# One-token sample projections in plain fp32 column groups, from weights fetched again, in a hybrid decoder layer

## What is computed

```python
def mixer_layer(x, c, start_pos, pool_buf, conv_buf, S0, chunked, ...):
    h = rms_norm(x, pre_norm_w) * (1.0 + scale[:, None]) + shift[:, None]
    proj = h @ w_in                       # 1024 -> 3080 columns
    u_a, z_a, qkv, z_b, b_raw, a_raw = jnp.split(proj, cuts, axis=-1)
    y_a, new_pool = pool_mix(u_a, pool_buf, start_pos, pool_w, pool_scale)
    ...                                   # short conv, gated delta rule, gates
    y = jnp.concatenate([y_a, y_b], axis=-1) @ w_out
    return x + gate[:, None] * rms_norm(y, post_norm_w), ...

yp, ... = mixer_layer(yp, c_prompt, 0, ..., True, *params)    # 2048 rows
ys, ... = mixer_layer(ys, c_sample, PAST_LEN, ..., False, *params)    # 8 rows
```

## Time and profile before

| | before |
|---|---|
| median of 3 runs | 1063.57 us (1062.31 to 1066.26) |
| the profiled execution, its own time | 1062.29 us |
| its span | 1060.5 us |
| TensorE busy | 1017.0 us, 96% |
| TensorE weight loads | 796.3 us, 75% |
| VectorE busy | 669.1 us, 63% |
| ScalarE busy | 363.8 us, 34% |
| GpSimd busy | 218.0 us, 21% |
| mean granted TensorE clock | 0.991 |
| HBM read, written | 156.43 MB, 44.81 MB |

### The profile page before, as it was taken

One profiled execution on the slowest core, in us unless ns is written; L12 is line 12 of the kernel. 1 busy time (PEld: TensorE's weight loads), 2 busy tenths in 40 slices (PEclk: granted clock), 3 DMA queues, 4 the chain that ended last, 5 costly groups with the idle time before them and its releaser, 6 DMA issues.

```text
span 1060.5 us, 16761 instructions
## 1 busy us (share of the span) xinstructions
PE 1017.0 (96%) x6235; PEld 796.3 (75%) x6235; DVE 669.1 (63%) x1392; ACT 363.8 (34%) x725; POOL 218.0 (21%) x222
## 2 busy tenths in 40 slices
PE   4999989999999999999999999999999999999995
PEld 1567667877777788887877788887877888888774
DVE  2479897577356795566356884676256775555644
ACT  5356322433714511322524511314426531121211
POOL 0133345565400101231000102230000100533000
PEclk9989999999999999999999999999999999999998
DMA  9696566364867553243756553244674343322265
GB/s 344 250 363 230 207 221 269 123 221 160 294 223 269 197 195 128 112 159 132 265 184 252 199 198 120 80 178 160 258 283 169 119 159 120 115 80 86 95 233 179
DMA packets 46803, 202.32 MB, mean 191 GB/s; under 512 B 9162, under 2 KB 9930, under 8 KB 29188
## 3 DMA queue, kind: packets, MB, share of 16 engines
q1 hardware_dynamic: 46724, 201.26, 51.8%
HBM read 156.43 MB, written 44.81 MB: 190 GB/s over the span
## 4 chain that ended last, share of the span: by engine, by line
PE 66%; DVE 1%; issue 1%; POOL 1%; ACT 0%; DVEq 0%; POOLq 0%; ACTq 0%
PE acc L2128 13%; PE acc L2130 12%; PE acc L2129 12%; PE ring L2178 9%; PE ring L2165 2%; PE acc L2165 2%; PE ring L2166 2%; PE ring L2167 2%; PE acc L2167 2%; PE acc L2166 2%; PE ring L2195 1%; PE ring L2204 1%; PE ring L2205 1%; PE ring L2365 1%; PE ring L2187 1%
## 5 line engine op out<-in xcount | busy, mean ns | idle before, releaser
L2128 PE MATMUL acc<-hhi,wsl 128*128 128x512 f32 x768 | 317.8, 414 | 4.8 <-DVE y L1367 4.7
L2130 PE MATMUL acc<-hhi,wsl 128*128 128x512 f32 x768 | 301.7, 393 | 0.0
L2129 PE MATMUL acc<-hlo,wsl 128*128 128x512 f32 x768 | 301.4, 392 | 0.0
L2128 PEld LDWEIGHTS acc<-hhi,wsl 128*128 128x128 f32 x768 | 145.7, 190 | 43.6 <-issue 10.6
L2130 PEld LDWEIGHTS acc<-hhi,wsl 128*128 128x128 f32 x768 | 145.1, 189 | 31.9
L2129 PEld LDWEIGHTS acc<-hlo,wsl 128*128 128x128 f32 x768 | 145.5, 189 | 27.8 <-issue 2.2
L1251 DVE SCALAR_TENSOR_TENSOR cacc<-raw,cw,cacc 128x512 f32<-128x512 f32 x144 | 114.8, 797 | 5.1
L1900 POOL TENSOR_TENSOR wsl<-wraw,wsl 128x512 fp32r<-128x512 f32 x60 | 84.1, 1418 | 107.7 <-ACT wsl L901 107.7
L934 ACT ACTIVATE raw<-acc 128x512 f32<-128x512 f32 x48 | 28.6, 597 | 140.6 <-PE acc L2130 140.5
L2165 PE MATMUL acc<-wsl,yhi 128*128 128x512 f32 x128 | 51.4, 401 | 5.0 <-DVE y L1367 3.4
L1248 DVE TENSOR_SCALAR cacc<-raw,cw 128x512 f32<-128x512 f32 x48 | 25.4, 529 | 47.1 <-ACT raw L934 44.3
(11 more groups left out here) (323 smaller groups left out, 1668.2 us busy)
## 6 DMA issues: line engine op xcount, KB each, us to landing
wsl<-kept_w SPq DMA_DIRECT2D x96, 1024.0 KB, 4.8
kept_w<-wsl SPq DMA_DIRECT2D x32, 1024.0 KB, 6.5
wraw<-in_w SPq DMA_DIRECT2D x64, 256.0 KB, 4.1
xb<-in_x SPq DMA_DIRECT2D x16, 512.0 KB, 5.7
wada<-in_w_ada SPq DMA_DIRECT2D x8, 1024.0 KB, 11.2
xres<-in_x SPq DMA_DIRECT2D x16, 512.0 KB, 5.7
out_y<-ytok SPq DMA_DIRECT2D x16, 512.0 KB, 8.1
xtr<-in_xt SPq DMA_DIRECT2D x12, 512.0 KB, 7.2
```

What stands on the lines that cost most here:

```text
L2128: nc.tensor.matmul(acc[t % 2][:], w[:, 0, k], hi[:, k], start=(k == 0), stop=False)
L2129: nc.tensor.matmul(acc[t % 2][:], w[:, 0, k], lo[:, k], start=False, stop=False)
L2130: last = nc.tensor.matmul(acc[t % 2][:], w[:, 1, k], hi[:, k], start=False, stop=(k == KT - 1))
```

## The change

In block 3 the raw fp32 weights of each of the 24 tiles are fetched a second time into two of the three `wraw` buffers, and the sample tile is computed from them: 8 plain fp32 matmuls with a stationary operand of 32 columns (`hpad`, the 8 sample rows padded with zeros). Contraction step k goes to the group of 32 output rows k % 4, so that each group sums two steps. ScalarE copies all 128 rows. The join multiplies the copy by `fold`, a matrix of four stacked identities, which transposes it and sums the groups, and VectorE only copies. `hs2` and the two operations that made it go; one clearing of `hpad` is added at the start, and a wait for constants at the start of VectorE's block 0. `spt` has one buffer instead of three and takes the room of the third raw buffer.

```diff
-        spt = over("spt", rw, 0, [2 * NS, WR, BT])
+        spt = over("spt", rw, 4 * KB, [P, BT])
...
-        hs2 = sb("hs2", [P, KT, 2 * NS], F32R)
+        hpad = sb("hpad", [P, KT, BS])
...
+            def sample_weights(t):
+
+                if t:
+                    sp.wait_ge(*done("pe", f"sp{t - 1}"))
+                else:
+                    sp.wait_ge(*split_done(NW - 1, 1))
+                for e in range(2):
+                    sp.dma_start(wraw[:, e], a["w"][t][:, e * (KT // 2):(e + 1) * (KT // 2)]).then_inc(raw_in[e], 16)
...
             def block_of(it, last=False):
                 enter(it)
                 if last:
+                    sample_weights(0)
                     sp.wait_ge(*h_hi(it, -1))
                     sp.wait_ge(*h_lo(it, -1))
...
                     elif t + WS < NW:
+                        if last and t == 0:
+                            sample_weights(1)
+                        if last and t + 2 < OUT:
+                            sample_weights(t + 2)
                         load_tile(it, t + WS)
...
-                if j == 0 and g >= WR:
-                    act.wait_ge(*done("pe", f"sc{g - WR}"))
-                nc.scalar.activation(spt[:, g % WR, j * P:(j + 1) * P], bank("sp", t)[0:2 * NS, 0:P], ACT.Copy).then_inc(*step("act", f"pj{t}"))
+                if j == 0 and g:
+                    act.wait_ge(*done("pe", f"sc{g - 1}"))
+                nc.scalar.activation(spt[:, j * P:(j + 1) * P], bank("sp", t)[:, 0:P], ACT.Copy).then_inc(*step("act", f"pj{t}"))
...
+            nc.vector.memset(hpad[:], 0.0)
...
-                    return nc.vector.tensor_reduce(pj[:, to:to + tiles.stop - tiles.start], turned[:, tiles], AX.X, ALU.add)
+                    return nc.vector.tensor_copy(pj[:, to:to + tiles.stop - tiles.start], turned[:, tiles])
...
-                nc.vector.tensor_copy(hs2[:, :, 0:NS], hs[:]).then_inc(*step("dve", "hh"))
-                dve.wait_ge(*done("dve", "hh"))
-                nc.vector.tensor_tensor(hs2[:, :, NS:], hs[:], hs2[:, :, 0:NS].bitcast(F32), ALU.subtract).then_inc(*step("dve", "hl"))
...
+                if it == 0:
+                    dve.wait_ge(s_prm2, 64)
...
             def sample_tile(it, t):
 
-                pe.wait_ge(*weights_in(it, t))
                 bank_free(pe, it, "sp", t)
-                w = wsl[:, slot(it, t)]
                 for k in range(KT):
-                    nc.tensor.matmul(bank("sp", t)[0:2 * NS, 0:P], hs2[:, k], w[:, 0, k], start=(k == 0), stop=False)
-                    last = nc.tensor.matmul(bank("sp", t)[0:NS, 0:P], hs2[:, k, 0:NS], w[:, 1, k], start=False, stop=(k == KT - 1))
+                    e, i = divmod(k, KT // 2)
+                    g = k % NBK
+                    if i == 0:
+                        pe.wait_ge(raw_in[e], 16 * (len(range(e, 2 * NW, WR)) + t + 1))
+                    last = nc.tensor.matmul(bank("sp", t)[g * BS:(g + 1) * BS, 0:P], hpad[:, k], wraw[:, e, i],
+                                            start=(k < NBK), stop=(k >= KT - NBK))
                 last.then_inc(*step("pe", f"sp{t}"))
...
-                    last = nc.tensor.transpose(bank("sc", g)[:, 2 * j * NS:2 * (j + 1) * NS], spt[:, g % WR, j * P:(j + 1) * P],
-                                               ident[0:2 * NS, 0:2 * NS])
+                    last = nc.tensor.matmul(bank("sc", g)[:, j * NS:(j + 1) * NS], spt[:, j * P:(j + 1) * P], fold[:, 0:NS],
+                                            start=True, stop=True)
```

More of the change, by code:

```diff
@@ L298 @@
     "pool": ["rx0", "rx", "clear", "half", "rk", "rstd", "ry0", "ry"],
-    "dve": (["xn", "h0", "h", "hh", "hl"] + ["g_a", "pg0", "g_beta", "g_sp", "g_g", "pg1", "g_d0", "g_d1"] + sample_plan_steps() + sample_out_steps() + ["ys1", "yn", "yr"]),
+    "dve": (["xn", "h0", "h"] + ["g_a", "pg0", "g_beta", "g_sp", "g_g", "pg1", "g_d0", "g_d1"] + sample_plan_steps() + sample_out_steps() + ["ys1", "yn", "yr"]),
 }
@@ L429, in layer_kernel @@
         rows96 = [t[0:GR * BS, j] for t in (tmpa, pooled) for j in range(2)]
-        fold = sb("fold", [GR * BS, 1 + NS])
+        fold = sb("fold", [P, 1 + NS])
         ssx = sb("ssx", [P, 4]); rx0 = sb("rx0", [P, 4]); rx = sb("rx", [P, 4])
@@ L443, in layer_kernel @@
         oss = sb("oss", [P, H]); on0 = sb("on0", [P, H]); on = sb("on", [P, H])
-        hs = sb("hs", [P, KT, NS])
+        hs = hpad[:, :, 0:NS]
         g8, s8 = sb("g8", [NS, 8, H]), sb("s8", [NS, 8])
@@ L1379, in sample_join @@
                     dve.wait_ge(*h_lo(it, -1))
-                turned = bank("sc", g)[:, 0:8 * NS].rearrange("p (t e s) -> p t s e", e=2, s=NS)
+                turned = bank("sc", g)[:, 0:4 * NS].rearrange("p (t s) -> p t s", s=NS)
                 def join(to, tiles):
-                    return nc.vector.tensor_reduce(pj[:, to:to + tiles.stop - tiles.start], turned[:, tiles], AX.X, ALU.add)
+                    return nc.vector.tensor_copy(pj[:, to:to + tiles.stop - tiles.start], turned[:, tiles])
                 if g < 4:
@@ L1564, in sample_rows @@
                 dve.wait_ge(*done("pe", "hs"))
-                nc.vector.tensor_tensor(hs[:], row_bank[:, 0:64].rearrange("p (k s) -> p k s", k=KT), amul[:, :, 1:1 + NS],
+                nc.vector.tensor_tensor(hs, row_bank[:, 0:64].rearrange("p (k s) -> p k s", k=KT), amul[:, :, 1:1 + NS],
                                         ALU.mult).then_inc(*step("dve", "h0"))
                 dve.wait_ge(*done("dve", "h0"))
-                nc.vector.tensor_tensor(hs[:], hs[:], mod[:, 0:8, 1:1 + NS], ALU.add).then_inc(*step("dve", "h"))
-                dve.wait_ge(*done("dve", "h"))
-                nc.vector.tensor_copy(hs2[:, :, 0:NS], hs[:]).then_inc(*step("dve", "hh"))
-                dve.wait_ge(*done("dve", "hh"))
-                nc.vector.tensor_tensor(hs2[:, :, NS:], hs[:], hs2[:, :, 0:NS].bitcast(F32), ALU.subtract).then_inc(*step("dve", "hl"))
+                nc.vector.tensor_tensor(hs, hs, mod[:, 0:8, 1:1 + NS], ALU.add).then_inc(*step("dve", "h"))
                 dve.wait_ge(s_const, 64)
@@ L2049, in turn_rows @@
                     last = nc.tensor.matmul(turn_bank[j // 2][:, 36 * (j % 2) + 9 * i:36 * (j % 2) + 9 * (i + 1)],
-                                            rows96[j][:, i * P:(i + 1) * P], fold[:], start=True, stop=True)
+                                            rows96[j][:, i * P:(i + 1) * P], fold[0:GR * BS], start=True, stop=True)
                 last.then_inc(s_tr, 1)
@@ L2292, in block_of @@
                         if t == 0:
-                            pe.wait_ge(*done("dve", "hl"))
+                            pe.wait_ge(*done("dve", "h"))
                             pe.wait_ge(s_pre, 3)
@@ L2467, in layouts @@
         "gsel": pick,
-        "fold": np.tile(np.concatenate([np.eye(1 + NS), np.zeros((BS - 1 - NS, 1 + NS))]), (GR, 1)).astype(np.float32),
+        "fold": np.tile(np.concatenate([np.eye(1 + NS), np.zeros((BS - 1 - NS, 1 + NS))]), (NBK, 1)).astype(np.float32),
         "c_all": np.concatenate([f("c_prompt"), f("c_sample")]).T.reshape(KT, P, 1 + NS).transpose(1, 0, 2),
```

## The result

| | before | changed |
|---|---|---|
| median (range) | 1063.57 us (1061.97 to 1066.26, 5 runs) | 1068.69 us (1067.96 to 1072.19, 5 runs) |
| ratio to before | | 1.005, 95% interval 1.0028 to 1.0072 |
| the profiled execution, its span | 1062.29, 1060.5 us | 1068.29, 1066.1 us |
| mean granted TensorE clock | 0.991 | 0.985 |
| HBM read | 156.43 MB | 169.01 MB |

The account below looks back on a forecast made before the run. TensorE was taken to pace block 3. Saving -4.1, first fetch +5.5, clock +1.2 and block 0 -0.2 gave +2.4 us on the profiled 1062.29 us, or 1066.0 us at the median; own range 1063.0 to 1069.5.

Parts of the forecast that it names:

- No difference to be told: Whole kernel: forecast 1066.0 us, within the 0.5% (5.3 us) that a measurement can't tell from no change.
- The bound: Block 3 is paced by TensorE: work taken off it shortens the kernel, delays lengthen it.
- The sample tile and the joins: Block 3 on TensorE: sample tiles save 5.1 us, joins cost 1.0 us more, net 4.1 us saved.
- the groups run together: Sample tiles: the four column groups' matmuls overlap, so eight take 0.46 us.
- the wait of the join behind sp12 for ScalarE: Block 3: this join waits for ScalarE's copy of sp11 and costs its full 0.5 us.
- rival 5: Sample tiles: groups don't run together, 1.76 us a tile, 24 us more, 1088 us; chance 0.02.
- The first fetch: Start of block 3: sp0 waits for raw halves issued late by SP; 5.5 us lost, bounds 3.0 to 10.
- The clock: Around the idling at sp0: granted TensorE clock falls to 0.50, costing 1.2 us, bounds 0 and 3.3.
- The later fetches: Block 3 after sp0: each lands in 2.4 to 4.1 us, wanted 5.5 us later at the least, so hidden.
- Rival 3: Block 3's dense stretches: every tile's fetch late, ten tiles lose 1 us each, sum near 1076 us; chance 0.12.
- no wait for `wraw` at tiles 1 to 23: Block 3, sign in the profile after: TensorE waits for raw weights only at the first sample tile.
- Block 0: Block 0: dropping two VectorE operations ahead of gg saves 0.2 us, up to 3.3 more if low clock is avoided.

Follow-up runs that it names:

- the second set: The changed kernel again, unchanged, on another chip beside the kernel before: median 1071.84 us, ratio 1.0082.
- Experiment 4: Changed kernel with the first raw fetch issued early in block 2, the 2 MB state moved to tile 8 and output rows split two and two: 1058.75 us, ratio 0.9961.
- experiment 2: Kernel before, with one added TensorE wait at the start of block 3 for cbuf and pbuf to land: ratio 1.010.
- experiment 6: Experiment 4 with a group's two steps issued one behind the other (the pairs): ratio 0.9972; with all eight steps in one group: 1.0239.
- experiment 5: Experiment 4 with late first fetch (first kernel): 1.0018; Experiment 4 with output rows together, only state moved: 0.9996; kernel before with both transfers moved: 0.9991.
- experiment 7: Kernel before, with VectorE's split of the sample input in block 0 moved behind gg: ratio 0.9987.
- experiment 3: Experiment 1's kernel with raw weights fetched for sp0 only and reused for sp1 to sp23: ratio 0.9959.
- experiment 1: Changed kernel with the first tile's raw halves issued earlier, in SP's loop of block 2: 1066.7 us, ratio 1.0032; second set 1.0039.

## Why the prediction was right, and where a size was off

**The forecast.** The first median, 1068.69 us, lies in the forecast's own range, 1063.0 to 1069.5 us, near its slow end; the second set's, 1071.84, lies over it. "No difference to be told" did not hold: both intervals leave out 1. The mechanism was right in its largest term, the late first fetch, but 2.4 us were forecast where 5.1 were measured. That the first median stayed inside the range is in part luck.

**The bound.** TensorE paces block 3: right. Experiment 4 leaves its waits at some 2 us, and the wait added at the front in experiment 2 went through to the end.

**The sample tile and the joins, -4.1 us.** Right, the size a little high. sp1 saves 0.23 (0.24 reckoned). Experiment 4, where little else is left of the change, is 0.39% faster, 4.1 us (2.6 to 5.7); its block 3 alone gives 2.7, and 3.7 with one fetch, so that part of the 4.1 us stands ahead of block 3. That the groups run together was the basis, and experiment 6 shows it. Right too was the wait of the join behind sp12 for ScalarE. Three sums of the prediction are slightly or plainly off: 24 x 1.01 is 24.2, a join costs 0.89 - 0.32 = 0.57 more, and rival 5's 1.76 us a tile against 0.46 makes 31 us more, not 24; experiment 6 measured 29 to 30.

**The first fetch, 5.5 us.** Right in place and mechanism, 5.9 us measured. With the low clock behind it, its lateness costs 6.1 us by the ratios and 7.8 by block 3 alone, with the transfers out of the way. The landing took 5.5 us after the issue, not the 4.8 and 5.0 of `cbuf` and `pbuf`. The 2.6 us estimated from the fit of the Trainium skill, "DMA: Bandwidth & Descriptors", section "Anatomy of one DMA", were too small here by a factor of two: 1 MB stood ahead, and the Trainium skill gives the fit for one DMA on GpSimd's path, while SP issues these. The shortest landing of a half fetched in block 3, 2.4 us, is near it.

**The clock, 1.2 us.** Too small in the profile of the changed kernel: the low stretch reached 4 us into the work, 2 us lost, within the bounds of 0 and 3.3. Experiment 2 shows that the idling brings it without the new sample tiles.

**The later fetches: "hidden".** This is the step that failed, and the largest part of what made +5.1 out of +2.4 us. The sentence set 2.4 to 4.1 us of landing against 5.5 us of time, and took the output rows and the state as "wanted much later". They are, but they stand in the same queue, and nothing in the sum asked what a fetch finds ahead of it. Behind 2 MB of output rows sp4's fetch took 7.0 us; experiment 5 prices the output rows at 2.0 us by block 3, 3.7 by the ratios. The wait itself is 0.4 us (by the 16 records: 0.99 against 0.64); most of the cost comes through the clock, which the prediction tied to longer waits only. Rival 3 had the mechanism, a fetch that lands too late for a single buffer, but at ten tiles; it came at one, and at sp1 as well when the first fetch was early. What the prediction held against rival 3, a DMA share of 0.22, was read from the quiet stretch 910 to 950; ahead of sp4 the trace of the kernel before has 0.94 (792 to 799), and that of the changed kernel 1.00 (799 to 804). The sign "no wait for `wraw` at tiles 1 to 23" failed at sp4.

**Block 0, -0.2 us.** Not settled: by experiment 7 between nothing and 3 us.

**The sum.** With the saving of experiment 3's block 3: -3.7 + 5.9 + 2.0 + 0.4 + 1.7 (the low clock at 808.9) - 0.9 (block 2's earlier end in this profile) = 5.4 of the 5.6 us between the two spans. With the 2.7 to 3.2 that experiment 4 gives (without and with its 0.5 us of waits for `wraw`) it would be 5.9 to 6.4, so the terms are known to about 1 us. Against the forecast of 2.4, the later fetches (2.1 instead of 0) are the largest difference, then the clock (0.8 more), the first fetch (0.4 more) and the saving (0.4 less), while the earlier end of block 2 gives 0.7 more back than the 0.2 reckoned for block 0.

## To carry to other kernels

Here a load was late by what stood ahead of it in its queue, not by its own size: the same 256 KB took 2.4 us at the least, 5.5 behind 1 MB, 7.0 behind the 2 MB of output rows, and 9.4 behind the state's 2 MB. Before a fetch is called hidden, put the landing of every transfer issued in the few microseconds ahead of it into the sum, and look where the issuing engine's own program stands when the data are wanted. A new stream of short-deadline fetches wants the large, patient transfers moved out of its way in the same edit; here, together with the earlier first fetch, this turned 5 us lost into 4 us won. Small fp32 matmuls with few stationary columns are worth spreading over the column groups: eight took 0.58 us instead of 1.87. And where the start of a kernel varies from one execution to the next, the length of the changed part alone, read from the profiles, tells small costs apart that whole times can't.

## What the runs showed that I had not expected

- The clock fell behind short waits, but not behind all. In four profiles (the change, twice, experiment 1, and experiment 5 with only the state moved) TensorE was 0.3 to 0.8 us late at sp4, in a stretch of small matmuls, and had 3.4 us at 0.50 behind it, so that half a microsecond of lateness cost 2. In the four in which sp4 was on time (experiments 3 and 4, the pairs of experiment 6, and experiment 5 with the late first fetch) it stayed at 1.00 there. But waits as short at a later tile left the clock at 1.00: 0.34 us at 855.2 in experiment 5's first kernel, and these two in experiment 4. That lateness at sp4 and the low clock go together is shown by eight profiles; why there and not later stays open.

```profile
843.71 0.43 PE L2222 MATMUL ring<-wraw,hpad 128*32 128x128 f32 x8 [0.29 <-DMA wraw<-in_w]
844.37 0.43 PE L2222 MATMUL ring<-wraw,hpad 128*32 128x128 f32 x8 [0.24 <-DMA wraw<-in_w]
```

- Two steps of one column group issued one behind the other cost only 0.02 us a tile more than in turn, though all eight in one group cost 1.29 us more.
- Two transfers of 2 MB had no measurable effect on the kernel before wherever they stood (0.9991, interval to 1.0005; block 3 the same to 0.1 us), and cost one that fetches just in time 5 us of block 3, 7 to 8 by the ratios.
